# Sums of squares on TensorE in two column groups of 64 tokens, without adding squares on VectorE

## The chip, the core and the metric

The kernel runs on one core of a Trainium2 chip. The core has TensorE (matrix products, PE in the profile, its weight loads PEld), VectorE (DVE), ScalarE (ACT), GpSimd (POOL) and SyncE (SP), which issues the weights' transfers. The time is that of one execution on the device in microseconds; a smaller time is better.

## The reference, cut to what matters

A block of five layers works on 256 tokens of width 1024. Each layer begins with a root-mean-square norm of x, and a last one gives the output:

```python
def rmsnorm(x, g):
    xf = x.astype(jnp.float32)
    y = xf * lax.rsqrt(jnp.mean(xf * xf, axis=-1, keepdims=True) + EPS)
    return (y * g.astype(jnp.float32)).astype(x.dtype)
# even layer:  x + gate * (y @ out_w)          mixer: x + g2 * (y_mix @ w_out)
# odd layer:   x + gate * (y @ out_w), then a norm with final_g
# feed-forward (before and behind the mixer):
#              x + 0.5 * g * ((silu(h @ w_gate) * (h @ w_up)) @ w_down)
# in the mixer y_mix = [rms_norm(y_conv), rms_norm(y_ssm)], each of width 512
# the end: rms_norm(x, final_norm)
```

The part at issue is `mean(xf * xf)`: for each token the sum of the squares of its 1024 values (512 in the mixer).

## The kernel before, in words

x is held transposed, `xT`: 128 partitions are channels, k = 0 to 7 are the eight groups of 128 channels, and 256 columns are the tokens. Weights come in pieces of 128 by 1024 values through a ring of ten slots (`ring`). SyncE issues the transfers in a fixed order and waits for a slot to be free. ScalarE rounds a piece to its high part `WH`, VectorE takes the difference as the low part `WL`, and TensorE multiplies in three products (high by high, low by high, high by low), which `mm3` and `mm3s` issue. Every engine has its program written out in order; semaphores connect them. The modulation vectors of later layers (`ada`) are summed on VectorE in between.

A layer's end goes like this. `out_rows` (line 666) accumulates the layer's output in `pacc`, 128 channels by 256 tokens for each of eight n. For the last unit it works by quarters q of two n each and calls `tail(q, h)` after each half. On VectorE `update` (line 1739) adds the two n of a quarter, times the gate, to `xT` (line 1750). ScalarE squares each `xT[:, n]` into `SQT[:, n]` (line 1207). The sum over channels is a matrix product in float32, issued by `stats` (line 648): the squares of 128 tokens are the stationary operand and ones the moving one, so the sums stand in PSUM with tokens as partitions, copied over the columns; m = 0 and 1 are the two halves of the tokens. `finish` (line 696) places these products. In the even layer, both feed-forward layers (F1, F2) and the mixer VectorE adds the squares of k = 1, 2 and 3 to those of k = 0 (`add_squares`, line 1744), so TensorE sums five k. In the odd layer (weights given, two kinds of sums: the moving operand is 1 and the squared gain of `final_g`) it sums all eight, four of them in the midst of the accumulation. The mixer's own two norms (`cs`, `ss`) sum four k each.

Then VectorE reads the sums (line 1685, in the odd layer 2029), finds the reciprocal root in eight small steps (to line 1702), TensorE spreads it over the partitions (`spread`, after some products with constants, `warm`, that keep it at work), and VectorE and ScalarE make the next layer's input (lines 1731, 1736).

```python
            def stats(pb, w, i, at, first, stop):
                p.wait_ge(s_sq, at + 1)
                n = pb.shape[1] // 2
                for m in range(2):
                    last = mm(pb[:, n * m:n * m + n], SQT[:, i, m * P:m * P + P], w, first and m == 0, stop)
```

Of the kernel before, what the change touches and what calls it, by code (L numbers as in the profile page):

```python
# [14 lines left out]
P = 128  # L15
# [218 lines left out]
def build(nc, I, out):  # L234
    ctx = ExitStack()
    with ctx:
# [3 lines left out]
        def sem(name):  # L240
            return ctx.enter_context(nc.semaphore(name))
# [27 lines left out]
        def v3(ap, a):  # L269
            return ap.rearrange("p (a n) -> p a n", a=a)  # L270
# [96 lines left out]
        s_grh, s_grl = sem("s_grh"), sem("s_grl")  # L367
        s_sq = sem("s_sq")
        s_sqr = sem("s_sqr")
        s_sqa = sem("s_sqa")  # L370
        s_r = sem("s_r")
        s_u = sem("s_u")
        s_hh = sem("s_hh")
# [129 lines left out]
        LAST_H = [None, "eg3", "sk3", "f1u10", "wb1"]  # L503
        X_FIN = {L_EVEN: 0, L_ODD: 8, L_F1: 24, L_MIX: 32, L_F2: 40}
        SQ_FIN = {L_EVEN: 0, L_ODD: 16, L_F1: 24, L_MIX: 40, L_F2: 48}
        SQA_FIN = {L_EVEN: 0, L_F1: 3, L_MIX: 6, L_F2: 9}
        OUTS = {L_EVEN: "eo", L_ODD: "oo", L_F1: "f1d", L_MIX: "wo", L_F2: "f2d"}
        TAIL = {L_EVEN: "eo7", L_ODD: "oo7", L_F1: "f1d10", L_MIX: "wo3", L_F2: "f2d10"}

# [18 lines left out]
        def _(eng):  # L528
# [31 lines left out]
            def mm(o, a, b, start=True, stop=True):  # L560
                return eng.matmul(o, a, b, start=start, stop=stop, skip_group_check=True)  # L561
# [86 lines left out]
            def stats(pb, w, i, at, first, stop):  # L648

                p.wait_ge(s_sq, at + 1)  # L650
                n = pb.shape[1] // 2
                for m in range(2):
                    last = mm(pb[:, n * m:n * m + n], SQT[:, i, m * P:m * P + P], w, first and m == 0, stop)
                last.then_inc(s_sqr, 1)
                sqr_n[0] += 1

# [38 lines left out]
            def finish(L, weights=None):  # L695
                st = {}

                def sums(q):
                    for k in (2 * q, 2 * q + 1):
                        w = ones if weights is None else weights[:, k, :].unsqueeze(2).to_broadcast([P, 2, 64])  # L700
                        stats(st["pb"][:, 0:256], w, k, SQ_FIN[L] + k, k == 0, k == 7)

                def tail(q, h):
                    if q == 0 and h == 0:
                        st["pb"] = open_(f"fin{L}", None, True)
                    if weights is not None and q >= 2 and h == 0:
                        sums(q - 2)
                    if q == 3 and h == 1:
                        if weights is None:
                            p.wait_ge(s_sqa, SQA_FIN[L] + 3)  # L710
                            stats(st["pb"][:, 0:256], ones, 0, SQ_FIN[L] + 3, True, False)
                        sums(2)
                        sums(3)
                        full[f"fin{L}"] = (s_sqr, sqr_n[0])
                return tail
# [386 lines left out]
            for half in range(2):  # L1102
                H, Lo = piece(2 * k + half, a)
                i = Y_G0 + half
                p.wait_ge(s_yl, i + 1)
                for n in range(4):
                    for kk in range(2):
                        sl = slice(n * P, n * P + P)
                        last = mm3(bks[n // 2][:, (n % 2) * T:(n % 2) * T + T], (H[:, kk, sl], Lo[:, kk, sl]),
                                   (YH[:, i % 3, kk, :], YL[:, i % 3, kk, :]), half == 0 and kk == 0 and n % 2 == 0,  # L1110
                                   half == 1 and kk == 1)
                    if half == 1 and n == 2:
                        spread("cr", 0, 6)
                last.then_inc(s_use, 1)
                if half == 0:
                    pb = open_("cs")
                    for n in range(4):
                        stats(pb[:, 0:256], ones, n, 32 + n, n == 0, n == 3)
                    full["cs"] = (s_sqr, sqr_n[0])
            full["gu0"] = full["gu1"] = used("glu")  # L1120

            def ssm_sums():
                pb = open_("ss")
                for n in range(4):
                    stats(pb[:, 0:256], ones, 4 + n, 36 + n, n == 0, n == 3)
                full["ss"] = (s_sqr, sqr_n[0])

            out_rows(L_MIX, "wo0", Y_C0, True, False, mid=ssm_sums)
# [493 lines left out]
        def _(eng):  # L1622
# [115 lines left out]

            def update(L, g):

                def add_squares(n):
                    v.wait_ge(s_sqa, SQA_FIN[L] + n - 1)
                    v.wait_ge(s_sq, SQ_FIN[L] + n + 1)
                    tt(SQT[:, 0, :], SQT[:, 0, :], SQT[:, n, :], ADD).then_inc(s_sqa, 1)

                for q in range(4):
                    v.wait_ge(*acc_done(L, q))
                    v.wait_ge(s_x, X_FIN[L])
                    for n in (2 * q, 2 * q + 1):
                        stt(out=xT[:, n, :], in0=pacc[:, n, :], scalar=g[:, n:n + 1], in1=xT[:, n, :],  # L1750
                            op0=MUL, op1=ADD).then_inc(s_x, 1)
                    if L != L_ODD and q < 2:
                        for n in ((1,), (2, 3))[q]:
                            add_squares(n)
                v.wait_ge(s_x, X_FIN[L] + 8)


# [263 lines left out]
            update(L_ODD, M1[:, 16:24])  # L2021


            pm = pw[place["fin1"]][:, 0:256:64].rearrange("p (m e) -> p m e", e=2)
            mod_cols(6, M2[:, 0:24], "ffn1_norm")
            v.wait_ge(*v.step(tt(GS, GS, fg, MUL)))
            v.wait_ge(*full["fin1"])
# [452 lines left out]
```

## Time and profile before

| | |
|---|---|
| median of 3 timed runs | 1000.13 us (999.41 to 1001.33) |
| the profiled execution | 997.22 us, span 995.50 us |
| TensorE busy | 963.5 us (97%), 8041 products |
| VectorE busy | 719.0 us (72%) |
| ScalarE busy | 510.0 us (51%) |
| granted clock of TensorE, mean | 0.997 |
| HBM | 219 GB/s over the span |

A row of the timeline gives the start and the length in us, the engine, the line, the operation, what it writes and reads, and, after x, how many equal ones follow one another; in brackets is how long the engine stood idle before, and for whom. `128*64 128x128` is a product with 128 rows and 64 columns stationary and 128 columns moving. A float32 product leaves two records of load and two of product. Products overlap, so their lengths do not add up; the distances between starts do.

### The profile page before, as it was taken

The page shows a single profiled execution, that of the slowest core. Times are in us where ns is not written, and L with a number is a line of the kernel's source. Part 1 is how long each engine was busy: PE and PEld are TensorE (multiplying, and loading weights), DVE is VectorE, ACT ScalarE, POOL GpSimd, SP SyncE. Part 2 cuts the span into 40 slices and gives each one's busy share as a digit, 9 for nine tenths or more (in the row PEclk, how much of TensorE's full clock was granted, in tenths as well). Part 3 has the DMA queues.
Part 4 walks back from the last instruction along what each step waited for, and adds up shares of the span by engine and source line. Part 5 has one row for each costly group of instructions (what it writes and reads, how often), then busy time and mean ns, then how long its engine had stood idle before and what let it go on. Part 6 is the DMA issues. An engine that isn't in the chain of part 4 may idle for free.

```text
span 995.5 us, 19242 instructions
## 1 busy us (share of the span) xinstructions
PE 963.5 (97%) x8041; PEld 943.3 (95%) x8041; DVE 719.0 (72%) x1006; ACT 510.0 (51%) x745; POOL 42.5 (4%) x68
## 2 busy tenths in 40 slices
PE   6999999989999999999999999999999999999998
PEld 5999999989999899999999999998999999999998
DVE  4778877767856766586899887978888766465554
ACT  4654364446544446644655366465555454444444
POOL 2100000000000004320100000000000000000000
PEclk9999999999999999999999999999999999999999
DMA  9987586744875894669268776776534357474731
GB/s 365 367 291 254 181 294 243 287 159 149 268 250 184 286 300 159 227 236 312 69 230 304 261 272 244 267 255 198 170 127 128 128 169 239 143 251 152 249 112 43
DMA packets 138990, 219.55 MB, mean 221 GB/s; under 512 B 7177, under 2 KB 110970, under 8 KB 138904
## 3 DMA queue, kind: packets, MB, share of 16 engines
q1 hardware_dynamic: 137152, 214.98, 62.8%
q0 software_dynamic: 992, 1.76, 0.7%
q10 hardware_dynamic: 760, 1.59, 0.4%
q8 instruction: 63, 1.03, 0.4%
q14 instruction: 23, 0.19, 0.1%
HBM read 217.25 MB, written 1.05 MB: 219 GB/s over the span
## 4 chain that ended last, share of the span: by engine, by line
PE 77%; DVE 11%; issue 4%; DMA 4%; ACT 3%; SPq 0%; ACTq 0%; DVEq 0%
PE pw L561 54%; PE pacc L561 22%; DVE WL L1635 2%; DVE ACC L1651 2%; DMA ring<-in_ada_w 1%; ACT AR L1158 1%; ACT WH L1158 1%; DMA ring<-in_odd_in_w 1%; DVE SQT L1731 1%; DVE hl L1736 1%; DMA cst<-in_consts 1%; ACT SQT L1158 1%; DMA ring<-in_ffn_w_down 0%; DMA ring<-in_odd_out_w 0%; DVE xT L1750 0%
## 5 line engine op out<-in xcount | busy, mean ns | idle before, releaser
L1158 ACT ACTIVATE WH<-ring 128x1024 fp32r<-128x1024 f32 x288 | 301.2, 1055 | 276.6 <-PE pw L561 136.2
L1635 DVE TENSOR_TENSOR WL<-ring,WH 128x1024 fp32r<-128x1024 f32 x288 | 347.4, 1224 | 88.0 <-ACT WH L1158 87.6
L561 PE MATMUL pw<-hh,WH 128*128 128x256 f32 x1408 | 373.4, 287 | 5.8 <-DVE WL L1635 3.1
L561 PE MATMUL pw<-hh,WL 128*128 128x256 f32 x1408 | 368.8, 283 | 0.0
L561 PE MATMUL pw<-hl,WH 128*128 128x256 f32 x1408 | 285.3, 284 | 0.0
L561 PEld LDWEIGHTS pw<-hh,WH 128*128 128x128 f32 x1408 | 270.5, 192 | 12.8 <-issue 7.9
L561 PEld LDWEIGHTS pw<-hh,WL 128*128 128x128 f32 x1408 | 271.1, 193 | 0.0
L561 PEld LDWEIGHTS pw<-hl,WH 128*128 128x128 f32 x1408 | 219.9, 192 | 0.2
L561 PE MATMUL pacc<-YH,WH 128*128 128x256 f32 x672 | 191.6, 285 | 3.1 <-issue 1.8
L561 PE MATMUL pacc<-YL,WH 128*128 128x256 f32 x672 | 190.2, 283 | 0.0
L561 PE MATMUL pacc<-YH,WL 128*128 128x256 f32 x672 | 190.2, 283 | 0.0
L561 PEld LDWEIGHTS pacc<-YH,WH 128*128 128x128 f32 x672 | 129.0, 192 | 5.7 <-issue 4.6
L1158 ACT ACTIVATE AR<-pw 128x512 f32<-128x512 f32 (+8 forms) x180 | 80.7, 465 | 97.6 <-PE pw L561 96.6
L561 PEld LDWEIGHTS pacc<-YL,WH 128*128 128x128 f32 x672 | 129.0, 192 | 0.0
L561 PEld LDWEIGHTS pacc<-YH,WL 128*128 128x128 f32 x672 | 129.0, 192 | 0.0
L1651 DVE SCALAR_TENSOR_TENSOR ACC<-ring,PC,ACC 128x1024 f32<-128x1024 f32 x95 | 121.7, 1281 | 2.5 <-DMA ring<-in_ada_w 2.3
L1681 DVE TENSOR_TENSOR YL<-AR,YH 128x512 fp32r<-128x512 f32 x48 | 32.8, 691 | 28.2 <-ACT YH L1158 28.1
L2173 DVE TENSOR_TENSOR AR<-AR,pw 128x256 f32<-128x256 f32 x44 | 16.5, 417 | 50.2 <-ACT AR L1158 50.1
L561 PE MATMUL pw<-WH,hh 128*128 128x256 f32 x192 | 50.7, 286 | 1.0 <-DVE WL L1635 0.9
L561 PE MATMUL pw<-WL,hh 128*128 128x256 f32 x192 | 50.2, 283 | 0.0
L1158 ACT ACTIVATE YH<-AR 128x512 fp32r<-128x512 f32 x48 | 29.8, 628 | 39.3 <-DVE AR L2173 22.7
L561 PE MATMUL pw<-AR 128*128 128x128 f32 (+6 forms) x416 | 42.2, 286 | 0.9 <-ACT AR L1158 0.8
(269 smaller groups left out, 793.9 us busy)
## 6 DMA issues: line engine op xcount, KB each, us to landing
ring<-in_w_mod SPq DMA_DIRECT2D x72, 512.0 KB, 4.6
ring<-in_odd_in_w SPq DMA_DIRECT2D x56, 512.0 KB, 6.1
ring<-in_ada_w SPq DMA_DIRECT2D x48, 512.0 KB, 6.7
ring<-in_ffn_w_gate SPq DMA_DIRECT2D x44, 512.0 KB, 4.6
ring<-in_ffn_w_up SPq DMA_DIRECT2D x44, 512.0 KB, 5.1
ring<-in_ffn_w_down SPq DMA_DIRECT2D x44, 512.0 KB, 4.9
ring<-in_even_in_w SPq DMA_DIRECT2D x40, 512.0 KB, 7.1
ring<-in_even_out_w SPq DMA_DIRECT2D x16, 512.0 KB, 6.0
```

The costliest lines, as they stand in the source:

```text
L561: return eng.matmul(o, a, b, start=start, stop=stop, skip_group_check=True)
L1158: return eng.activation(dst, src, func, **kw)
L1635: tt(WL[:, i % NL, :], slot(half_of(i)), WH[:, i % NH, :].bitcast(F32), SUB).then_inc(s_lo, 1)
L1651: stt(out=acc, in0=slot(g), scalar=wc, in1=acc, op0=MUL, op1=ADD).then_inc(s_ada, 1)
L1681: tt(f2(YL[:, i % 3]), src, f2(YH[:, i % 3]).bitcast(F32), SUB).then_inc(s_yl, 1)
L1731: stt(out=SQT[:, k, :], in0=xT[:, k, :], scalar=GS[:, k:k + 1], in1=rb, op0=MUL, op1=MUL).then_inc(s_u, 1)
L1736: stt(out=hl[:, q, :], in0=SQT[:, q, :], scalar=m[:, q:q + 1], in1=hh[:, q, :].bitcast(F32), op0=ADD, op1=SUB).then_inc(s_hl, 1)
L2173: tt(fbuf(blk, m), fbuf(blk, m), pw[b][:, T:2 * T], MUL).then_inc(s_bank[b], 1)
```

## The change

`stats` no longer keeps the squares of 128 tokens stationary with 128 columns of ones moving. It keeps 64 tokens stationary with 64 columns moving, and writes them to the lower and the upper 64 partitions by turns, that is, to the two column groups of the array. The product for one k is now four instructions instead of two. In the odd layer the two moving vectors fill 32 columns each. `add_squares` and its semaphore are gone; in its place `finish` sums k = 0 to 3 too, right behind the last accumulating product, ahead of k = 4 to 7.

```diff
@@ stats
-                n = pb.shape[1] // 2
                 for m in range(2):
-                    last = mm(pb[:, n * m:n * m + n], SQT[:, i, m * P:m * P + P], w, first and m == 0, stop)
+                    for r in (slice(0, 64), slice(64, P)):
+                        last = mm(pb[r, P * m:P * m + 64], SQT[:, i, P * m + r.start:P * m + r.stop], w,
+                                  first and m == 0, stop)
@@ finish
-                        w = ones if weights is None else weights[:, k, :].unsqueeze(2).to_broadcast([P, 2, 64])
+                        w = ones[:, 0:64] if weights is None else weights[:, k, :].unsqueeze(2).to_broadcast([P, 2, 32])
...
                         if weights is None:
-                            p.wait_ge(s_sqa, SQA_FIN[L] + 3)
-                            stats(st["pb"][:, 0:256], ones, 0, SQ_FIN[L] + 3, True, False)
+                            sums(0)
+                            sums(1)
                         sums(2)
                         sums(3)
@@ cs, and alike ss
-                        stats(pb[:, 0:256], ones, n, 32 + n, n == 0, n == 3)
+                        stats(pb[:, 0:256], ones[:, 0:64], n, 32 + n, n == 0, n == 3)
@@ update
-                def add_squares(n):
-                    v.wait_ge(s_sqa, SQA_FIN[L] + n - 1)
-                    v.wait_ge(s_sq, SQ_FIN[L] + n + 1)
-                    tt(SQT[:, 0, :], SQT[:, 0, :], SQT[:, n, :], ADD).then_inc(s_sqa, 1)
...
-                    if L != L_ODD and q < 2:
-                        for n in ((1,), (2, 3))[q]:
-                            add_squares(n)
@@ the odd layer's sums, as VectorE reads them
-            pm = pw[place["fin1"]][:, 0:256:64].rearrange("p (m e) -> p m e", e=2)
+            pm = v3(pw[place["fin1"]][:, 0:256], 2)[:, :, 0:64:32]
```

VectorE at the end of the even layer, before: `xT<-pacc,MOD,xT` is an update of x, `SQT<-SQT` an add of squares, `RS<-pw` the first step of the norm.

```order
L1657 STREAM_TRANSPOSE ACC<-pw 128x256
L1658 TENSOR_TENSOR MOD<-ACC,VC 128x8
L1750 SCALAR_TENSOR_TENSOR xT<-pacc,MOD,xT 128x256 x2
L1744 TENSOR_TENSOR SQT<-SQT 128x256
L1750 SCALAR_TENSOR_TENSOR xT<-pacc,MOD,xT 128x256 x2
L1744 TENSOR_TENSOR SQT<-SQT 128x256 x2
L1750 SCALAR_TENSOR_TENSOR xT<-pacc,MOD,xT 128x256 x4
L1685 TENSOR_SCALAR RS<-pw 128x2
```

And VectorE at the same place after the change:

```order
L1656 STREAM_TRANSPOSE ACC<-pw 128x256
L1657 TENSOR_TENSOR MOD<-ACC,VC 128x8
L1744 SCALAR_TENSOR_TENSOR xT<-pacc,MOD,xT 128x256 x8
L1684 TENSOR_SCALAR RS<-pw 128x2
L1694 TENSOR_SCALAR RS<-RS 128x2
```

The three adds between the updates are gone; the eight updates stand in one run. The same holds in both feed-forward layers and in the mixer.

TensorE at the end of the even layer, before (`pw<-cst,SQT` are the sums of squares, `pw<-cst,RS` the spreading, `pw<-cst` products with constants):

```order
L561 MATMUL pacc<-YH,WH 128x256
L561 MATMUL pacc<-YL,WH 128x256
L561 MATMUL pacc<-YH,WL 128x256
L561 MATMUL pw<-cst,SQT 128x128 x10
L561 MATMUL pw<-cst,RS 128x128 x2
L561 MATMUL pw<-cst 128x128 x4
L561 MATMUL pw<-hh,WH 128x256
```

And TensorE there after the change:

```order
L559 MATMUL pacc<-YH,WH 128x256
L559 MATMUL pacc<-YL,WH 128x256
L559 MATMUL pacc<-YH,WL 128x256
L559 MATMUL pw<-cst,SQT 64x64 x32
L559 MATMUL pw<-cst,RS 128x128 x2
L559 MATMUL pw<-cst 128x128 x4
L559 MATMUL pw<-hh,WH 128x256
```

Ten instructions of 128 columns by 128 became thirty-two of 64 by 64, eight k instead of five, at the same place.

## Rows read from the trace of the kernel before

**Rows 1.** The page, the chain that ended last, by engine.

```profile
PE 77%; DVE 11%; issue 4%; DMA 4%; ACT 3%; SPq 0%; ACTq 0%; DVEq 0%
```

**Rows 2.** Timeline, even layer's end, TensorE and VectorE: start, us, engine, line, operation.

```profile
210.21 0.28 PE L561 MATMUL pacc<-YH,WL 128*128 128x256 f32 x1
211.43 2.89 PE L561 MATMUL pw<-cst,SQT 128*128 128x128 f32 x20 [0.94 <-DVE SQT L1744]
...
210.49 0.88 DVE L1744 TENSOR_TENSOR SQT<-SQT 128x256 f32<-128x256 f32 x2 [0.17 <-ACT SQT L1158]
211.29 1.65 DVE L1750 SCALAR_TENSOR_TENSOR xT<-pacc,MOD,xT 128x256 f32<-128x256 f32 x4
214.43 0.16 DVE L1685 TENSOR_SCALAR RS<-pw 128x2 f32<-128x2 f32 x1 [1.49 <-PE pw L561]
```

**Rows 3.** Timeline, end of F1: the last accumulating product and the norm.

```profile
683.05 0.28 PE L561 MATMUL pacc<-YH,WL 128*128 128x256 f32 x1
...
686.11 0.16 DVE L1685 TENSOR_SCALAR RS<-pw 128x2 f32<-128x2 f32 x1 [1.29 <-PE pw L561]
```

**Rows 4.** Timeline, end of the mixer, the same two.

```profile
786.62 0.28 PE L561 MATMUL pacc<-YH,WL 128*128 128x256 f32 x1
...
790.23 0.16 DVE L1685 TENSOR_SCALAR RS<-pw 128x2 f32<-128x2 f32 x1 [1.29 <-PE pw L561]
```

**Rows 5.** Timeline, end of F2: the same two, products behind the sums, output copies.

```profile
985.88 0.28 PE L561 MATMUL pacc<-YH,WL 128*128 128x256 f32 x1
...
988.43 1.28 PE L561 MATMUL pw<-cst 128*128 128x128 f32 x10
988.70 0.16 DVE L1685 TENSOR_SCALAR RS<-pw 128x2 f32<-128x2 f32 x1 [1.49 <-PE pw L561]
...
990.62 1.62 DVE L2375 TENSOR_SCALAR AR<-pw,RS 128x512 f32<-128x512 f32 x2 [0.31 <-PE pw L1145]
```

**Rows 6.** Timeline, end of the odd layer: last accumulating product, last squares, norm.

```profile
473.62 0.28 PE L561 MATMUL pacc<-YH,WL 128*128 128x256 f32 x1
...
474.46 0.81 ACT L1158 ACTIVATE SQT<-xT 128x256 f32<-128x256 f32 x2 [1.53 <-DVE xT L1750]
...
476.20 0.16 DVE L2029 TENSOR_SCALAR RS<-pw 128x2 f32<-128x2 f32 x1 [0.97 <-PE pw L561]
```

**Rows 7.** Timeline, TensorE, the mixer's second sum and the second product behind it.

```profile
764.38 1.95 PE L561 MATMUL pw<-cst,SQT 128*128 128x128 f32 x16
...
766.29 0.28 PE L561 MATMUL pacc<-YL,WH 128*128 128x256 f32 x1
```

**Rows 8.** Eight loads of 64 columns (timeline); then groups: xcount | busy, mean ns.

```profile
271.45 0.54 PEld L561 LDWEIGHTS pw<-AR 128*64 128x64 f32 x8
...
L561 PE MATMUL pw<-AR 128*64 128x64 f32 x16 | 1.4, 228 | 0.0
L561 PEld LDWEIGHTS pw<-AR 128*64 128x64 f32 x16 | 1.1, 137 | 0.2
```

**Rows 9.** Timeline, products of 64 columns in two column groups by turns, with neighbours.

```profile
721.30 0.28 PE L561 MATMUL pw<-hl,WH 128*128 128x256 f32 x1
721.51 0.20 PEld L561 LDWEIGHTS pw<-AR 128*64 128x64 f32 x4
...
721.51 2.84 PE L561 MATMUL pw<-AR 128*64 128x128 f32 x48
724.28 0.39 PE L561 MATMUL pw<-hh,WH 128*128 128x256 f32 x1
```

**Rows 10.** Timeline behind the mixer's first sum: low part, and the product that needs it.

```profile
755.30 0.68 DVE L1681 TENSOR_TENSOR YL<-AR,YH 128x512 fp32r<-128x512 f32 x1
756.13 0.36 PE L561 MATMUL pw<-YH,WH 128*128 128x256 f32 x1
```

**Rows 11.** Stretches: busy and count of PE, PEld, DVE, ACT, POOL; PEclk, DMA share, GB/s.

```profile
215.00:235.00 20.00, 18.39 (x148) 17.21 (x149) 15.26 (x31) 12.53 (x19) 0.80 (x1) 1.00 0.20 58
327.00:332.00 5.00, 4.85 (x28) 4.85 (x29) 4.83 (x11) 1.25 (x3) 0.00 (x0) 0.66 0.48 151
```

More of the change, by code:

```diff
@@ L369, in build @@
         s_sqr = sem("s_sqr")
-        s_sqa = sem("s_sqa")
         s_r = sem("s_r")
@@ L505, in build @@
         SQ_FIN = {L_EVEN: 0, L_ODD: 16, L_F1: 24, L_MIX: 40, L_F2: 48}
-        SQA_FIN = {L_EVEN: 0, L_F1: 3, L_MIX: 6, L_F2: 9}
         OUTS = {L_EVEN: "eo", L_ODD: "oo", L_F1: "f1d", L_MIX: "wo", L_F2: "f2d"}
@@ L1124, in ssm_sums @@
                 for n in range(4):
-                    stats(pb[:, 0:256], ones, 4 + n, 36 + n, n == 0, n == 3)
+                    stats(pb[:, 0:256], ones[:, 0:64], 4 + n, 36 + n, n == 0, n == 3)
                 full["ss"] = (s_sqr, sqr_n[0])
```

## The prediction

> **What bounds the kernel now.** I read the chain that ended last first: TensorE holds 77% of it, VectorE 11% [rows 1]. The median of a 128x256 product is not its price, since products overlap; its price is the distance between starts, 0.12 us in the accumulations. So a change pays where TensorE stands still or does work that can shrink. Next I read the timeline of the five layer ends (even, odd, F1, mix, F2). There all the squares of a layer must be summed before VectorE can begin the norm, whose result everything behind waits for. In the even layer's end the last accumulating product starts at 210.21 and the norm at 214.43, 4.22 us later [rows 2]. In between the reader sees two things. TensorE idles 0.94 us for VectorE's adding of squares, and VectorE, busy with two adds at 210.49 (0.88 us), takes up the remaining updates of x only at 211.29, though the product of the third quarter started long before. The last squares follow those updates. The other ends: 3.06 us in F1 [rows 3], 3.61 in mix [rows 4], 2.82 in F2 [rows 5]. In the odd layer, whose update has no adds, 2.58 [rows 6].
>
> **Prices.** A float32 product is two records of load and product. With 128 columns stationary the sums run at (1.95 - 0.28) / 15 = 0.112 us per record, so one k (two products, four records) costs 0.45 us [rows 7]; the 0.28 is the length of the last record. After the change a k is four products of 64 stationary and 64 moving columns, eight records, in four pairs: one record in each column group. What does a pair cost? The trace holds two near relatives, and they are the bounds:
> - One column group alone, 64 by 64 columns: eight loads in 0.54 us, each 0.137 long, so (0.54 - 0.137) / 7 = 0.058 us per record; the products are 0.22 long (mean 0.228, with two openers that are longer) [rows 8].
> - Two column groups by turns, but 128 columns moving: 48 records in 2.84 us, (2.84 - 0.27) / 47 = 0.055 each, a pair 0.109 [rows 9].
>
> In the second the loads of the two groups overlap: four of them end 0.20 us after the first began [rows 9]. At 0.058 behind one another, each 0.137 long, they would take 0.31. And twice 64 moving columns take half the stream of twice 128. So I take 0.058 us for a pair (the 64 by 64 row, the other group beside it) and keep 0.109 as the upper end. Below 0.058 nothing is possible, since each group by itself needs that. A k then costs 0.23 instead of 0.45.
>
> The way in and out costs extra. In: from the last full-width product to the first 64-wide one 0.21 us (721.30 to 721.51) where 0.12 is usual, so 0.09, and the first load lies open, 0.05 more (half of the 0.11 that a 128-column load costs there, next sentence) [rows 9]. Out: the full-width product behind starts at 724.28, 0.07 before the 64-wide group's end (721.51 + 2.84 = 724.35). A 64-moving product is 0.22 long, so 0.15 after its start. The full-width product is 0.39 long instead of 0.28: its load lies open, 0.11 [rows 9]. Both ways together are about 0.3 us, more than one k saves and less than two.
>
> **Layer ends without adds (even, F1, mix, F2).** Removed: three adds of about 0.43 us in each, twelve in all, and the waits around them. Added: three more k in the sum, eight instead of five. From the last accumulating product: 0.21 in, 0.05 open load, 31 x 0.058 = 1.80 for 32 pairs, and from the last product's start to the norm. That is now 0.11 beyond the group's end (211.43 + 2.89 = 214.32, norm 214.43), and with 0.22 for the product 0.33 [rows 2, 8]. Sum 2.39 us.
>
> Does anything else end later? The odd layer shows a VectorE without adds: the squares are through at 474.46 + 0.81 = 475.27, 1.65 after the last product [rows 6]. TensorE reaches the last k at 0.21 + 0.05 + 28 x 0.058 = 1.88. So TensorE is late, by 0.2 us, and the squares are ready. Savings: even 4.22 - 2.39 = 1.83, F1 0.67, mix 1.22, F2 0.43. Of the last only 0.2 reaches the output: there VectorE's copies wait for TensorE's transposes, not for the norm [rows 5], and TensorE comes out of the sums 988.43 - (985.88 + 2.06 + 0.15) = 0.34 earlier less 0.11 open load.
>
> **The odd layer.** Two excursions of two k in the midst of products: before, eight records at 0.112 and one product at 0.12, 1.02 us from the first sum to the second product behind. After: 0.09 + 0.05 + 7 x 0.058 + 0.15 + 0.11 + 0.12 = 0.93, so 0.09 each. At its end the last k waits for the last square (475.27): 475.27 + 0.05 for the signal + 0.05 + 3 x 0.058 + 0.33 = 475.87 instead of 476.20, so 0.33. Together 0.5.
>
> **The mixer's two sums.** The second stands in the accumulation with four k: 766.29 - 764.38 = 1.91 before [rows 7]; after 0.09 + 0.05 + 15 x 0.058 + 0.38 = 1.39, so 0.52, with PE at work before and behind. The first saves as much by itself, but the products behind it need a low part that VectorE finishes at 755.30 + 0.68 = 755.98, and they start at 756.13 already [rows 10]. That is 0.1.
>
> **Sum.** 1.83 + 0.67 + 1.22 + 0.2 + 0.5 + 0.52 + 0.1 = 5.0 us. The saving must not come back later: in 215 to 235 the DMA engines are busy 0.20 at 58 GB/s, so the weights for the next stage are in and their transfers wait for slots, not for memory [rows 11]. Slots, splits and products all follow the norm, so the whole moves forward. The profiled execution took 997.22 us (span 995.50 and 1.7 around it) and would take 992.2. It lies 2.9 under the median of the timed runs, 1000.13; applied to that median the forecast is 995.1.
>
> **Rivals.**
> 1. *Loads and products of the two groups take turns.* Then the pair is at its upper end, 0.109. An end with eight k takes 0.26 + 31 x 0.109 + 0.33 = 3.97: even gains 0.25, F1 loses 0.91, mix 0.36, F2 1.15 (1.1 at the output). Odd: 0.09 + 0.05 + 0.76 + 0.38 = 1.28 against 1.02, twice 0.26, less 0.17 at its end. The second mixer sum 0.09 + 0.05 + 1.64 + 0.38 = 2.16 against 1.91, the first 0.2. Together 2.9 slower: 1003.0. It decides from a pair of about 0.09 us on (124 steps from pair to pair in the four ends and 44 elsewhere: 5.0 / 168 = 0.03 above 0.058). Against it speak the overlapping loads and the pair of 0.109 with twice the columns, which is just the stream, loads hidden [rows 9]. The Trainium skill, "TensorE: Matmul & The Clock Gate", section "The mechanism" (of its Part 3), says that loads overlap products in flight only where the row group differs; here all rows are used and only the column groups differ. By that rule a pair would be a load behind a product, and the sum would be this rival's. The trace disagrees so far: in rows 9 loads of column groups do run beside products. No row shows it with 64 columns moving.
> 2. *The saving is taken back in the next stage*, because VectorE or the weight stream bounds it on its own account. For it: VectorE has 11% of the chain. Against it: it waits for the norm like all others, and the DMA share after the even end. If only F2, the mixer's sum and a little were left, 1.0: 999.1.
> 3. *TensorE's clock.* In 327 to 332 the granted clock is 0.66, that is, a stretch at 1.2 GHz after a wait of TensorE [rows 11]. 0.34 x 5 / 0.5 = 3.4 us at the low level cost up to 1.7 us. The change shifts all later waits by 2 us, so this stretch may go, or another come: 995.1 -/+ 1.7.
> 4. *VectorE stays late although the adds are gone*, because it comes to the updates late for other reasons: each end then gives perhaps half, 997.0.
>
> **Chances.** Forecast 0.70, rival 1 0.06, rival 2 0.10, rival 3 0.09 (half each way), rival 4 0.05. A measurement of this kernel tells 0.2% (2.0 us) from no change. Faster than 998.1: the forecast, rival 3 and rival 4, with a little off for noise, 0.83. Same: 0.11. Slower: 0.06. The range goes from 993.3 (the clock's stretch gone) to 998.9 (rival 2 nearly whole); rival 1 lies outside.
>
> **What would show it.** Right: sums of 32 products as one group with pairs 0.058 apart; norm 2.4 us behind the last accumulating product in even, F1 and mix; four updates of VectorE in unbroken pairs; no adds; TensorE's idle time for them gone. Wrong: pairs further apart than 0.09; the last square later than the seventh k; a new wait between the even end and 270 us; in the odd layer's middle the second product later than 1.02 us.

## The result, and the profile after

The changed kernel took 993.21 us (median of 4 executions, 991.34 to 993.49), the kernel before 1000.46 in the same comparison: ratio 0.9926, 95% interval 0.9912 to 0.9940, so 7.3 us faster. The forecast was 995.1 us with a range from 993.3: the direction was right, the size too small by 2 us, and the time lies 0.1 us outside the range.

| us | before | after | forecast for after |
|---|---|---|---|
| profiled execution, its span | 997.22, 995.5 | 993.12, 991.4 | 992.2 |
| last accumulating product to norm: even, F1, mix, F2 | 4.22, 3.06, 3.61, 2.82 | 2.41, 2.41, 2.42, 2.42 | 2.39 |
| the same in the odd layer | 2.58 | 2.27 | 2.25 |
| mixer's second sum, from the last product ahead to the second behind | 2.03 | 1.52 | 1.51 |
| timed median | 1000.46 | 993.21 | 995.1 |

First the even layer's end in the timeline of after (start, us, engine, line, operation), where [rows 2] stood before:

```profile
210.21 0.28 PE L559 MATMUL pacc<-YH,WL 128*128 128x256 f32 x1
210.41 1.95 PEld L559 LDWEIGHTS pw<-cst,SQT 128*64 128x64 f32 x64
210.42 2.08 PE L559 MATMUL pw<-cst,SQT 128*64 128x64 f32 x64
210.53 0.88 DVE L1744 SCALAR_TENSOR_TENSOR xT<-pacc,MOD,xT 128x256 f32<-128x256 f32 x2 [0.33 <-PE pacc L559]
211.04 0.81 ACT L1157 ACTIVATE SQT<-xT 128x256 f32<-128x256 f32 x2 [0.40 <-DVE xT L1744]
...
212.62 0.16 DVE L1684 TENSOR_SCALAR RS<-pw 128x2 f32<-128x2 f32 x1 [1.22 <-PE pw L559]
```

The reader is to see three things. The adds and TensorE's 0.94 us of idle time for them are gone; all 64 records run in one piece behind the last accumulating product. The 64 loads take 1.95 us, which is 32 pairs at 0.06; the first pair alone takes longer. And the last squares, at 211.04 + 0.81 = 211.85, are ready 0.65 us before TensorE ends (210.42 + 2.08 = 212.50): the matrix engine is what is late, as forecast. The ends of F1, mix and F2 are alike to 0.01 us, and the odd layer's norm comes 2.27 us behind its last product (timeline of after, odd, F1, mix, F2; they answer to [rows 3 to 6]):

```profile
472.60 0.28 PE L559 MATMUL pacc<-YH,WL 128*128 128x256 f32 x1
...
474.87 0.16 DVE L2020 TENSOR_SCALAR RS<-pw 128x2 f32<-128x2 f32 x1 [0.67 <-PE pw L559]
...
681.69 0.28 PE L559 MATMUL pacc<-YH,WL 128*128 128x256 f32 x1
...
684.10 0.16 DVE L1684 TENSOR_SCALAR RS<-pw 128x2 f32<-128x2 f32 x1 [1.02 <-PE pw L559]
...
784.03 0.28 PE L559 MATMUL pacc<-YH,WL 128*128 128x256 f32 x1
...
786.45 0.16 DVE L1684 TENSOR_SCALAR RS<-pw 128x2 f32<-128x2 f32 x1 [1.02 <-PE pw L559]
...
982.09 0.28 PE L559 MATMUL pacc<-YH,WL 128*128 128x256 f32 x1
...
984.51 0.16 DVE L1684 TENSOR_SCALAR RS<-pw 128x2 f32<-128x2 f32 x1 [1.22 <-PE pw L559]
```

The mixer's second sum, TensorE's timeline (it answers to [rows 7], where the product ahead started 0.12 us before the sum; 763.69 less 762.17 is 1.52 us, and the full-width product behind is 0.39 long, as estimated):

```profile
762.17 0.28 PE L559 MATMUL pacc<-YH,WL 128*128 128x256 f32 x1
762.38 1.15 PE L559 MATMUL pw<-cst,SQT 128*64 128x64 f32 x32
763.46 0.39 PE L559 MATMUL pacc<-YH,WH 128*128 128x256 f32 x1
763.69 0.28 PE L559 MATMUL pacc<-YL,WH 128*128 128x256 f32 x1
```

From F2's last product to the end of the span it is 9.60 us before and 9.28 after, so the output gains 0.3 where 0.2 was forecast. So every term of the sum came out within about 0.1 us, and the terms say 5 us. Yet the two profiled executions differ by 4.1 us and the medians by 7.3. The chain of waits shows why the first number is not 5. Besides the transfers at the start and one near 249 us that took as long in both (4.82 and 4.77 us), it has three weight transfers on it (start, us, what), each the first of several issued together after VectorE has freed a place in the ring; behind the first stands a stretch of 344 records without a wait. Before:

```profile
320.94 4.54 DMA ring<-in_odd_in_w
...
327.15 42.83 PE pw L561 x344
...
412.49 4.54 DMA ring<-in_odd_out_w
...
567.61 4.82 DMA ring<-in_ffn_w_down
```

After:

```profile
319.04 5.14 DMA ring<-in_odd_in_w
...
325.86 42.83 PE pw L559 x344
...
411.19 4.99 DMA ring<-in_odd_out_w
...
566.30 4.75 DMA ring<-in_ffn_w_down
```

The transfers took 13.90 us before and 14.88 after: 1.0 us of the 5.1 saved was lost to them in this pair of executions. The change edits nothing about them; it only lets them start earlier. Whether they scatter from execution to execution, and by how much, takes more profiles of both kernels.

### The profile page after: what moved, and what is told of

Read it like the earlier page. It is cut to its first block, busy times and chain, and to the rows that moved or that the text cites. A ratio compares the mean times of both kernels' runs of the same rounds, so it can differ in the third digit from the quotient of the medians.

```text
span 991.4 us, 19695 instructions
## 1 busy us (share of the span) xinstructions
PE 959.3 (97%) x8281; PEld 938.3 (95%) x8281; DVE 714.9 (72%) x994; ACT 509.2 (51%) x745; POOL 42.4 (4%) x68
## 3 DMA queue, kind: packets, MB, share of 16 engines
HBM read 217.25 MB, written 1.05 MB: 220 GB/s over the span
## 4 chain that ended last, share of the span: by engine, by line
PE 79%; DVE 10%; DMA 4%; issue 4%; ACT 3%; SPq 0%; ACTq 0%; DVEq 0%
PE pw L559 54%; PE pacc L559 24%; DVE ACC L1650 2%; DVE WL L1634 2%; DMA ring<-in_ada_w 1%; ACT AR L1157 1%; DMA ring<-in_odd_in_w 1%; DVE SQT L1730 1%; DVE hl L1735 1%; ACT WH L1157 1%; DMA cst<-in_consts 1%; DMA ring<-in_odd_out_w 1%; DMA ring<-in_ffn_w_down 0%; DVE AR L1650 0%; ACT hh L1157 0%
```

## The experiments

All runs with a median were timed against the kernel before on the same chip (its median in the five comparisons, e1 to e4, e5 to e8, e9 to e12, e13 to e16, e17 and e18: 1000.36, 999.57, 999.89, 1000.90, 1000.04).

**Both kernels again (no edit).**

> The kernel before, unchanged, for the spread of its runs and the granted clock of each. The changed kernel came out 7.3 us below it where 5.0 were forecast, while the two profiled executions are only 4.1 apart, and the mean clock of the changed kernel's runs is 0.998 with about 993.3 us, 1.0 with 991.3. Theory A (the rest is TensorE's clock): the runs near 1000 have a mean clock of about 0.995 (two or three stretches at the low level in the middle), one near 997 has 0.997, and the time falls by about 1.7 to 2 us for each stretch less. Rival B (the rest is in the work itself): all runs have the clock 0.997 of the profiled execution, whatever their time.

> The changed kernel, unchanged, beside it. Theory A: runs at clock 0.998 take 993 us, runs at 1.0 take 991.3, and at an equal number of low stretches it is 4.0 to 5.0 us under the kernel before. Rival B: about 7 us under it at equal clock.

Measured: before 1000.01 us (ratio to itself 0.9996, 0.9982 to 1.0011), after 993.37 (0.9941, 0.9921 to 0.9960). The gap of the medians, 7 us, is real. Theory A as e1 states it did not come out: it wanted a mean clock of about 0.995 near 1000 us, and the twelve executions had 0.996 to 0.998. Rival B wanted one clock for all, and didn't come out either; in the kernel after, the execution at clock 1.0 is the fastest again (992.12 us). The new profile of before is that of an execution of 1001.18 us, 4 us slower than the first. All its layer ends are as before (4.22, 2.58, 3.06, 3.60, 2.82). Its chain is not:

```profile
320.89 6.98 DMA ring<-in_odd_in_w
...
329.55 43.34 PE pw L561 x344
...
415.39 5.73 DMA ring<-in_odd_out_w
```

The four transfers that are issued together at 321 us also took longer to issue in e1 than in before (SyncE's timeline, before first); in the other profiles with this wait it is 2.1 to 2.5 us, and 2.94 in e12:

```profile
320.94 2.12 SPq L2446 DMA_DIRECT2D ring<-in_odd_in_w  x4
```

```profile
320.89 3.09 SPq L2446 DMA_DIRECT2D ring<-in_odd_in_w  x4
```

6.98 + 5.73 + 4.77 for the third is 17.48 us, 3.58 over the first profile, and the stretch of products behind the first transfer is 43.34 us. In an execution without low clock it is 41.35 (e2), so 42.83 and 43.34 hold 1.5 and 2.0 us of TensorE at 1.2 GHz.

**One half of the change alone.** e3 keeps the adds and takes the column groups; e4 drops the adds and keeps 128x128 products:

```
 e3:  for r in (slice(0, 64), slice(64, P)): mm(pb[r, P*m:P*m+64], SQT[...], w, ...)   # adds kept
 e4:  - p.wait_ge(s_sqa, ...); stats(..., 3, ...)   + sums(0); sums(1)                 # adds gone
```

> The sums of squares in two column groups with 64 columns, but VectorE still adds k = 1 to 3 (five k in the ends of even, F1, mix, F2). By the forecast's prices: the ends still wait for the last square behind the adds, so each norm comes only 0.44 us earlier (F2: 0.13 at the output), odd 0.5, the mixer's sums 0.6: 2.6 us faster than before. If the parts simply added up (theory: each is worth what it saves alone) it would have most of the 5 us.

> No adds on VectorE, but the sums with 128 tokens stationary and 128 columns moving as before (eight k in each of the four ends). From the last accumulating product to the norm: 0.12 + 31 x 0.112 + 0.38 = 3.97 us in each: even 0.25 earlier, F1 0.91 later, mix 0.36 later, F2 1.15 later; 2.2 us slower than before. Rival: the adds by themselves cost the even layer 1.8 us and mix 1.2, so leaving them out alone is already faster.

Measured: e3 996.79 us (0.9966, 0.9954 to 0.9977), e4 1002.01 (1.0026, 1.0015 to 1.0038). Timeline of e3, even end:

```profile
210.22 0.28 PE L561 MATMUL pacc<-YH,WL 128*128 128x256 f32 x1
211.43 0.45 PE L561 MATMUL pw<-cst,SQT 128*64 128x64 f32 x8 [0.93 <-DVE SQT L1745]
212.27 1.63 PE L561 MATMUL pw<-cst,SQT 128*64 128x64 f32 x32 [0.39 <-ACT SQT L1159]
214.02 0.16 DVE L1686 TENSOR_SCALAR RS<-pw 128x2 f32<-128x2 f32 x1 [1.07 <-PE pw L561]
```

And of e4:

```profile
210.28 0.28 PE L561 MATMUL pacc<-YH,WL 128*128 128x256 f32 x1
210.40 3.74 PE L561 MATMUL pw<-cst,SQT 128*128 128x128 f32 x32
...
214.25 0.16 DVE L1685 TENSOR_SCALAR RS<-pw 128x2 f32<-128x2 f32 x1 [2.77 <-PE pw L561]
```

Each half leaves the other's limit standing. With the adds kept, TensorE waits 0.93 and 0.39 us for VectorE and ScalarE whatever its own pace, and the end falls from 4.22 only to 3.80. Without adds but at 0.112 us a record, eight squares take 3.74 us: the even end gains 0.25, F1, mix and F2 (3.96 each) lose. By the rows of all ends e3 gains 2.6 to 2.7 us and e4 loses 2.1, as expected (2.6 and 2.2); the medians say 3.6 and 1.7, and both halves together 7. The parts are not additive: three more squares cost 0.45 us each at the old pace and 0.23 at the new one, and the new pace is of use only where no add has to be waited for.

**Idle products against the low clock.** e5 and e6 put five idle products into the even end's wait and nine ahead of the first product behind the weight transfer, to keep TensorE at work there:

```
+ warm(5, "warm1a")                                       # before the norm's spreading
+ for _ in range(9): mm(pb[:, 0:P], ident, ones)          # cols_T("og7"), behind open_(name)
```

> The kernel before, with idle products in two waits of TensorE: five (1.1 us) between the sums of the even layer and the spreading of its norm, and nine (2.0 us) before the first product that waits for a weight transfer near 326 us, where a stretch at 1.2 GHz has followed in five of the six profiles. Theory A (the clock is part of the gap of the medians: before runs at a mean granted clock of 0.9969, after at 0.9982, and 0.001 of clock goes with 0.9 us over the 75 timed executions): the clock comes to 0.999 or more and the time falls by 1.3 to 2.8 us, to 997.6 to 999.1. Theory B (the gap is in the weight transfers of the odd layer, and the low stretches fall where TensorE has slack or are replaced by waits for transfers): the time stays within 0.5 us of before, 999.9 to 1000.9, whatever the clock.

> The changed kernel with the same idle products in the same two waits. Theory A: it had fewer low stretches to lose, so it gains less, 0.7 to 1.6 us, to 991.7 to 992.7, and the difference between the two kernels with idle products is that of the rows, 5 to 6 us instead of 7. Theory B: 993.3 within 0.5 us, and the difference of the two stays 7 us. In both, the sum of the two transfers on the chain in the odd layer (9.1 to 12.7 us so far) is no different for the two kernels if it is only scatter; if it is the change that shortens them, it is above 11 for the kernel before and below 10.5 for this one.

Measured: 1002.13 (1.0027, 1.0015 to 1.0040) and 996.00 us (0.9969, 0.9958 to 0.9980): both 2.6 slower than without, which neither theory expected. TensorE's timeline of e6 shows my mistake:

```profile
323.29 0.64 PE L559 MATMUL pw<-ACC,cst 128*32 128x256 f32 x8
326.18 3.90 PE L559 MATMUL pw<-cst 128*128 128x128 f32 x18 [2.25 <-ACT AR L1158]
329.81 0.39 PE L559 MATMUL pw<-hh,WH 128*128 128x256 f32 x1
```

(A low stretch stood there in four of the six profiles so far, not in five.) The nine stood behind the wait for a free accumulator, not in it, and began when the real products could have: 3.6 us on the path. They ran in the low stretch themselves: 18 records take 3.90 us here and 2.28 in e10. So the pair says nothing for or against the clock, but it is a pair at equal terms: its gap is 6.1 us. In e9 and e10 the nine stand one step earlier, ahead of the adaptive sum:

```
  p.wait_ge(*ada_done(8 * c + 7))
+ for _ in range(9 if key == "og7" else 0): mm(pb[:, 0:P], ident, ones)
```

> e5 again with its nine idle products moved: there they stood behind TensorE's wait for a free accumulator and began at the moment when the real products could (326.18 in e6), 3.6 us on the path. Here they stand ahead of that wait, before the adaptive sum that TensorE makes at about 325 us, where it has 2.5 us to wait in any case and VectorE takes the sum 5 us later. Theory A (low stretches are part of the gap): no stretch at 1.2 GHz near 215 or 327 us, the product stretch behind it 41.35 us and not 42.83, a median 1.3 to 2.0 us under that of before. Theory B (low stretches come anyway, later, or cost nothing in the end): within 0.5 us of before.

> The changed kernel with the same idle products in the same places. Theory A: it gains less than e9 does, 0.5 to 1.5 us (991.7 to 992.7 where before stands at 1000), and the difference of the two kernels with idle products is 5 to 6 us. Theory B: no gain, the difference stays at 6.1 (e5 against e6) to 7 us.

Measured: before with idle products 999.06 us (0.9993, 0.9983 to 1.0004), after with them 991.68 (0.9918, 0.9905 to 0.9931; 4 runs, 991.60 to 991.80). TensorE's timeline of e10:

```profile
322.99 2.28 PE L559 MATMUL pw<-cst 128*128 128x128 f32 x18
325.19 0.64 PE L559 MATMUL pw<-ACC,cst 128*32 128x256 f32 x8
325.76 0.39 PE L559 MATMUL pw<-hh,WH 128*128 128x256 f32 x1
```

The wait is filled, the real product starts when it did, and the granted clock of the stretch is full. The rows of the two kernels, after and e10 (busy and count of PE, PEld, DVE, ACT, POOL; clock, DMA share, GB/s):

```profile
325.00:333.00 8.00, 7.14 (x47) 7.14 (x48) 7.83 (x14) 2.81 (x4) 0.00 (x0) 0.79 0.56 168
```

```profile
325.00:333.00 8.00, 8.00 (x71) 7.47 (x70) 7.83 (x14) 3.83 (x6) 0.00 (x0) 1.00 0.56 168
```

47 records became 71 in the same 8 us. Eleven of these only moved into the window (the last three idle ones and the eight of the adaptive sum); of the products behind the wait there are 60 instead of 47, and 59 in e2, which had the full clock without idle products. For the changed kernel the idle products seem worth 1.6 us, at the upper end of theory A (0.5 to 1.5). For the kernel before it was 0.8, with an interval from 1.7 faster to 0.4 slower, against 1.3 to 2.0 expected by theory A and under 0.5 by theory B: that decides neither. The gap between the two grew to 7.4 us instead of shrinking to 5 or 6, which speaks against the clock as the reason; but it rests on four executions of e10.

**What is left: the transfers.** e12 is before once more, e13 and e14 are e9 and e15 is e10 again, for their profiles.

> The kernel before, unchanged, for a third profile and for the scatter of its runs. If the two transfers on the chain of the odd layer are what makes it slower than its first profile (9.08 us together there, 12.71 in e1, 9.7 to 10.7 in those of the other kernels), they take 10 us or more here, and the time of the execution is 995.7 us plus what they take over 9.08 plus 1.5 us for a stretch at 1.2 GHz, within 0.5. If the excess is elsewhere, that sum misses by more.

> e9 again, for its profile. Without low stretches its time is 996.0 us (995.7, what is left of three profiles of before when the three weight transfers on the chain stand at 13.90 us and the low stretches are taken off, and 0.3 for the idle products in the even end) plus what the three transfers take over 13.90. Theory T (the transfers carry the rest of the gap, and are longer in the kernel before): they take 16 us or more. Theory S (they are scatter, alike in both kernels): 14.5 to 15.5 us as in after.

> As e13: by theory T three transfers of 16 us or more and a time of 998 us or more, by theory S 14.5 to 15.5 us and 996.6 to 997.6.

> e10 again, for its profile: 990.7 us plus what the three transfers take over 13.90; by both theories 14.5 to 15.5 us and 991.3 to 992.3.

Measured: e12 999.54 us (0.9999, 0.9985 to 1.0013), its profiled execution 1000.56; e13, e14 and e15, one execution each, 999.32, 998.20 and 993.81, so the same two kernels as e9 and e10 are 4.4 to 5.5 us apart here. The chain of e12:

```profile
320.98 6.76 DMA ring<-in_odd_in_w
...
329.42 43.32 PE pw L561 x344
...
415.24 4.99 DMA ring<-in_odd_out_w
...
570.77 4.98 DMA ring<-in_ffn_w_down
```

The two transfers of the odd layer took 11.75 us, more than the 10 expected. Its expectation for the time was 995.7 + (11.75 - 9.08) + 1.5 = 999.9 within 0.5, and it missed by 0.7. With the third transfer too (16.73 - 13.90), and with the 2.0 us that the stretch of 43.32 shows instead of 1.5, it is 1000.5, measured 1000.56. These two terms were put in after the result. Taking both off each profiled execution (time, less the three transfers over 13.90, less the 344 records over 41.34) gives what the kernel itself takes. Three of the executions below have a low stretch near 216 us as well (granted clock 0.57 in 214 to 222 in e3, 0.76 in 215 to 222 in e4 and e17). What it cost is read from the even norm to the transfer near 250 us, 35.3 us in the three profiles of before, and 36.85, 35.94 and 35.84 in those three:

| | time | transfers | 344 records | near 216 us | what is left |
|---|---|---|---|---|---|
| before | 997.22 | 13.90 | 42.83 | | 995.7 |
| before, e1 | 1001.18 | 17.48 | 43.34 | | 995.6 |
| before, e12 | 1000.56 | 16.73 | 43.32 | | 995.8 |
| after | 993.12 | 14.88 | 42.83 | | 990.7 |
| after, e2 | 992.12 | 15.32 | 41.35 | | 990.7 |
| groups only, e3 | 995.56 | 14.88 | 41.34 | 1.54 | 993.0 |
| no adds only, e4 | 1001.74 | 15.50 | 42.82 | 0.63 | 998.0 |
| one group, 64 wide, e17 | 1002.48 | 16.57 | 42.83 | 0.53 | 997.8 |

Three executions of before agree to 0.2 us and two of after to 0.1, and the difference is 5.0 us, the sum of the forecast. The halves come out as their expectations said, e3 2.7 under before (2.6 expected) and e4 2.3 over it (2.2).

The distances in the timelines say the same with nothing taken off (us; three profiles of before, two of after). The 0.6 us in the mixer's row are its two sums; of the first row's difference 0.2 us are the odd layer's sums in the middle.

| from | to | before, e1, e12 | after, e2 |
|---|---|---|---|
| even norm | odd layer's last product | 259.19, 263.19, 262.34 | 259.98, 258.35 |
| odd norm | F1's last product | 206.85, 206.77, 206.98 | 206.82, 207.21 |
| F1's norm | mixer's last product | 100.51, 100.51, 100.53 | 99.93, 99.92 |
| mixer's norm | F2's last product | 195.65, 195.62, 195.65 | 195.64, 195.64 |

The three profiled executions of before lie 7.0 us above the two of after on average, as the medians do. What goes beyond 5.0 lies in the odd layer, in the first row, and in two columns of the table above: its two transfers took 11.2 us on average in before (9.08, 12.71, 11.75) and 10.15 in after, 1.0 us more, and its low stretch cost 1.8 against 0.75, 1.1 us more. So by five profiles the 7 us are 5.0 of the change itself, 1.0 of transfers and 1.1 of low clock behind them.

The kernels with idle products confirm this only in part. On all three transfers together before took 16.0 us (3 profiles); after, e2, e7, e8, e15 and e16 took 15.2 (14.7 to 15.6). In e9, e10, e13 and e14 the first transfer is not on the chain, so theory T's 16 us for the three can't be read there; the other two took 11.6, 10.7 and 10.9 us in e9, e13 and e14, and 9.9, 10.2 and 10.1 in e10, e15 and e16, again about 1 us longer in the kernel before. e13 and e14 came to the 998 us and more that theory T wanted, but e13 with a low stretch in the mixer (granted clock 0.72 in 762 to 768; from F1's norm to the mixer's last product 102.02 us instead of 100.5). By their sum (996.0 us, the two transfers over 9.36, 1.5 for e13's stretch) e9, e13 and e14 should have taken 998.3, 998.8 and 997.5 us; they took 999.12, 999.32 and 998.20, 0.5 to 0.9 more, which no row explains. That speaks for theory T, but weakly.

e15 (expected 991.3 to 992.3) missed by 1.5 us. Its three transfers took 15.56 us, and the one near 249 us, which takes 4.6 to 4.9 in all other profiles in which it is on the chain, took 6.10. Over after that is 1.66 + 1.33, and 990.7 + 3.0 = 993.7, measured 993.81. The transfer in e10 and in e15:

```profile
247.97 4.64 DMA ring<-in_odd_in_w
```

```profile
248.00 6.10 DMA ring<-in_odd_in_w
```

Why the transfers should land later in the kernel before isn't settled: e3, e4 and e11 reach the first of them as late as before does and had 5.30, 5.07 and 5.05 us, so the moment alone is not it. The long ones are two of the three profiles of before; the first profile has the shortest three of all. Chance in so few profiles is not excluded for this split; for the gap of the medians (7.3 and 7.0 us in two comparisons) it is far less likely.

**The pace of the sums.** e7: four groups of 32 tokens; e8 and e11: 32 and 128 columns of ones with the two groups; e17: 128 tokens at once, 64 columns, no adds; e18: four groups, 128 columns.

```
 e7:  for r in (slice(0, 32), slice(32, 64), slice(64, 96), slice(96, P)): ...
 e8:  mm(pb[r, P*m:P*m+32], SQT[...], ones[:, 0:32], ...)
 e11: mm(pb[r, P*m:P*m+128], SQT[...], ones[:, 0:128], ...)
 e17: mm(pb[:, P*m:P*m+64], SQT[:, i, m*P:m*P+P], ones[:, 0:64], ...)
 e18: e7 with 128 columns
```

> The changed kernel with four column groups of 32 tokens instead of two of 64, all sums with 64 columns moving as before. Theory C (within a column group a load and its product follow each other, the groups work beside each other: 64 columns in and 64 through are 0.053 us of the 0.058 measured for a pair): four products together take 32 in and 64 through, 0.040 to 0.045 us, a block of one square 0.17 instead of 0.233 us; then the last square of VectorE (211.85 against a last product at 212.28) sets four of the ends, which gain 0.2 us each, the mixer's two sums 0.25 each and the odd layer 0.5 together: 991.5 us, clock aside. Theory D (loads go one after the other and take 29 ns each whatever their columns, the products are hidden behind them): four take 0.117 us, a block 0.47 us, and the kernel is slower than after by 8 x 0.23 us in four ends and as much again elsewhere, 1002 us. Theory E (loads go one after the other and take their columns, 128 for a square's half either way): nothing changes, 993.3 us.

> The changed kernel with 32 columns of ones moving instead of 64, two groups of 64 tokens as before (the weighted sums of the odd layer move 2 x 16). Theory C (load and product in series within a group): 64 in and 32 through, 0.040 to 0.045 us a pair, and the same gains as with four groups, 991.5 us. Theories D and E (the loads, one after the other, set the pace): the pair stays at 0.058 us and the time at 993.3 us.

> The changed kernel with 128 columns of ones moving through each group of 64 tokens, where after has 64; e8 with 32 left the pair at 0.058 us. Theory F (the loads of the two groups, 64 columns each, set the pace one after the other, and the products lie beside them): the pair is 0.058 us still as long as a product of 128 columns (0.053) fits beside the two loads (0.053), and the time stays at after's, 993.3. Theory G (a group can't take its next load until its own product is through): 64 in and 128 through are 0.080 us a pair, 0.088 more per square, 0.7 us more in each of four ends and 0.35 in each of the mixer's sums and 0.5 in the odd layer: 997.3. Rival 1 of the forecast (the groups take turns): 0.107 us a pair, 1003.

> The changed kernel with the 128 tokens of a half stationary at once again (no column groups), but 64 columns of ones moving as in after, no adding of squares. Theory C2 (without groups a load and its product follow each other, 128 columns in and 64 through): 0.085 us a product against 0.112 in before and 0.058 a pair in after, 0.34 us a square instead of 0.233; with eight squares 0.85 us more in each of four ends, 0.4 in each of the mixer's sums and 0.4 in the odd layer, 998 us. Theory N (the columns that move are all that counts, the groups are for nothing): 0.058 us a product, each end 2.4 us from the last accumulating product to the norm, and 993.3 us, or a little less without the change of the tile position.

> Four column groups of 32 tokens with 128 columns moving, for the pace alone: two groups took 0.109 us a pair with 128 columns, 0.058 with 64 and with 32, four groups 0.056 with 64. If the products of 128 columns in neighbouring groups take turns two by two, four take 0.109 us as two did, and the ends are 4.0 us as in e11, 1002 us; if it is the loads of 64 columns that a product of 128 holds up, four loads of 32 fit better and the four take 0.067 to 0.08 us, the ends 2.7 to 3.1 us, 995 to 997 us; if each product waits for the one before, they take 0.21 us and the time is 1014 us.

Measured: e7 993.51 us (0.9939, 0.9925 to 0.9953), e8 993.92 (0.9945, 0.9930 to 0.9960), e11 1002.28 (1.0021, 1.0012 to 1.0031), e17 1001.33 (1.0008, 0.9998 to 1.0019), e18 1002.65 (one execution). The rows of the even end, one kernel to a fence, e7, e8, e11, e17, e18 (timeline: start, us):

```profile
210.37 1.99 PE L559 MATMUL pw<-cst,SQT 128*32 128x64 f32 x128
```

```profile
210.34 2.06 PE L559 MATMUL pw<-cst,SQT 128*64 128x32 f32 x64
```

```profile
210.75 3.71 PE L559 MATMUL pw<-cst,SQT 128*64 128x128 f32 x64
```

```profile
210.53 3.68 PE L559 MATMUL pw<-cst,SQT 128*128 128x64 f32 x32
```

```profile
210.64 3.70 PE L559 MATMUL pw<-cst,SQT 128*32 128x128 f32 x128
```

Each covers the same eight squares in 32 steps of 128 tokens, so the step can be read off:

| stationary tokens x groups | columns moving | step, us | kernel |
|---|---|---|---|
| 128 x 1 | 128 | 0.112 | before, e4 |
| 128 x 1 | 64 | 0.112 | e17 |
| 64 x 2 | 128 | 0.109 | e11 |
| 64 x 2 | 64 | 0.058 | after |
| 64 x 2 | 32 | 0.058 | e8 |
| 32 x 4 | 64 | 0.056 | e7 |
| 32 x 4 | 128 | 0.109 | e18 |

One reading fits all seven: the groups work side by side, within a group loads and products overlap, and the step is the longer of the two, a load of 0.112 us for 128 columns and 0.058 for 64, a product of 0.109 for 128 and at most 0.056 for 64. The reading was made after the runs, and none tests it anew. Theory C fell (e8 would have been faster), theories D and E fell (e7 and e8 bear E out, but e11's 0.109 with the same loads doesn't). So did F and G, which wanted 0.058 and 0.080 us for e11, C2, which wanted 0.085 for e17, and N: halving the columns alone (e17) gives nothing, nor does halving the tokens alone (e11). It takes both. Of e18's three cases the first came, 0.109. e11 also is rival 1 of the forecast made real: at 0.109 a pair it came to 1002.3 us, where that rival said 1003.0.

**The version the experiments point to.** Four groups and the idle products of e10:

> The changed kernel with four column groups of 32 tokens and the idle products of e10. The four groups took 0.07 us off each end in e7 and 0.5 us off the profile once transfers and clock are taken off; with the 1.6 us of e10 that is 991.2 us (990.8 to 991.7). A rival: the four groups give nothing in the median, as in e7 (993.51), and it is e10's 991.7.

Measured: 992.52 us (0.9925, 0.9910 to 0.9940), outside the 990.8 to 991.7 expected and no better than e10. Four groups save 0.07 us at an end (2.34 instead of 2.41), too little to see. The best version is e10, the changed kernel with idle products in two waits, 991.68 us; its interval (0.9905 to 0.9931) overlaps with that of after in the first comparison, and e15 was slower, so its 1.6 us over after is likely, not certain.

## Why the prediction was right, and where it was not

- **Price of a pair.** Forecast 0.058 us, measured 0.058. The lower bound [rows 8] held and the upper one [rows 9] did not apply, for the reason given: 128 columns moving set that row's pace, as e11 shows.
- **Layer ends.** Forecast 2.39, measured 2.41 in all four; VectorE ready before TensorE. Rival 4 is refuted: it comes to the updates in time once its adds are gone.
- **Odd layer.** 2.27 at its end for 2.25; an excursion in its middle 0.09 us shorter, as forecast (from the product ahead to the second behind 1.14 before, 468.83 to 469.88 after, 1.05).
- **Mixer's sums.** The second 1.52 for 1.51, a saving of 0.51 for 0.52. The first: behind it the shift against before grows only from 2.01 to 2.09 us, the 0.1 that the low part [rows 10] leaves.
- **Not taken back.** Rival 2 is refuted: the shift of 1.8 us from the even end reaches 319 us whole, and what is lost from there on is lost at two transfers whose length has its own scatter.
- **Rival 3**, the clock, is part of it: the pair of profiles has the same stretch near 327 us (42.83 us both), but over all executions after has the higher mean clock, and the profiles put 1.1 us of the gap there.
- **Rival 1** is refuted for after and confirmed as a price by e11. The Trainium skill, "TensorE: Matmul & The Clock Gate", section "The mechanism", says that loads overlap products in flight only where the row group differs. The trace disagrees: all rows are in use, 64 loads take 1.95 us while products of 0.22 us run, and the step of 0.058 leaves no room for a load and a product in turn. The same section of the Trainium skill also lets a load go ahead when it targets a background weight buffer; no run here shows whether that is what happens.
- **The step that failed** is the last of the sum: "It lies 2.9 under the median of the timed runs, 1000.13; applied to that median the forecast is 995.1." It took the profiled execution's distance from its median for a constant that the change would keep. In after that distance is 0.1 us. The kernel before scatters over 7 us (997.0 to 1004.2 in over 100 executions) and after over 3.4 (991.3 to 994.7 in 10). The forecast knew one source, the clock, and gave it 1.7 us to both sides; it didn't know that three transfers on the chain take 13.9 to 17.5 us, and that the profile in hand had the shortest of all. The runs showed in its place: 5.0 us like for like, 1.0 us of transfers and 1.1 us of low clock, both in the odd layer. The 2.9 should have stood as a term that might shrink by 2 or 3, and the range would have begun at 992. (As written the range begins at 993.3; its terms, 995.1 less 1.7, give 993.4.)

What stays open is why the 2 us beyond 5.0 came. Over all executions a lower mean clock goes with longer times (before: 52 runs at 0.998 have a median of 998.8 us, 57 at 0.997 one of 1000.6, 10 at 0.995 one of 1002.9; after: 6 at 0.998 one of 993.4, 2 at 1.000 one of 991.7), which leaves 5.4 us at equal clock, near the 6.0 of the profiles; but e9 against e10, both with hardly any low stretch, differ by 7.4. The two don't go together, and I don't choose between them.

## What to carry to other kernels

When two edits remove two limits of the same wait, price them together: alone, one was worth 3.6 us and the other cost 1.7. A profile is one execution; before its time is subtracted from anything, see which transfers and low-clock stretches lie on its chain and compare it with the scatter of the timed runs. In this kernel narrow float32 sums paid only when stationary and moving columns were both cut. Idle products against the low clock must stand in the wait they are to fill: behind it they cost 2.6 us here; in it they gained 0.8 and 1.6, neither quite clear of noise.

## What the runs showed of the hardware

- The step of float32 products with few columns is the longer of load (0.112 us for 128 stationary columns, 0.058 for 64) and product (0.109 for 128 moving, at most 0.056 for 64), with column groups side by side: seven combinations above. I had expected a group of its own to add the two.
- Records of the two groups start 6 to 7 ns apart and then 52 ns pass to the next pair; with four groups all four start within 20 ns.
- A weight transfer that is issued with three others took 4.54 to 6.98 us to land, at the same place in the same kernel (before, e1); issuing the four took 2.1 and 3.1 us.
- A stretch at 1.2 GHz near 327 us followed TensorE's wait of 1.6 to 4.0 us in 9 of 12 profiles without idle products there, and in none of the six with idle products in the wait. It cost 1.5 us, and 2.0 in e1 and e12, where the wait was longest (4.0 and 3.8 us). The length of the wait alone doesn't decide: it came behind 1.56 us (before) and not behind 2.32 (e3), where a low stretch near 216 us had gone before, nor behind 2.00 (e2).
